# Fifth gate pair as split products inside attention, and the softmax maximum taken off in the exponential

## The chip, the cores and the metric

The kernel runs on one core of a Trainium2 chip. The metric is the device time of one execution in microseconds (us). The kernel before takes 1711.48 us, the median of three runs that lie between 1711.03 and 1711.93.

The engines are named as in the profile: PE is the matrix engine (PEld its weight loads, which overlap its products), DVE the vector engine, ACT the scalar engine, POOL the general one, SP the engine that only starts transfers. Each engine runs its own instructions in the order in which they are written, and waits at semaphores for the others.

## The reference

One decoder layer on 256 tokens of width 2048, all in fp32. What matters here is its first half:

```python
h = rms_norm(x, attn_norm_w)
q, k, v, z, gates = split(h @ w_in)              # gates: 2 x 2048 columns
# branch A: 16 query heads, 4 key heads, window 128, blocks of 128
scores = q @ k.T * 64**-0.5 - slope[head] * dist # -inf outside the window
m = max(max(scores, axis=-1), sink[head])
p = exp(scores - m)
attn = (p / (sum(p) + exp(sink[head] - m))) @ v
# branch B: RWKV-7 time mixing of z, gives y
merged = sigmoid(gates[0]) * (attn @ w_branch_a) + sigmoid(gates[1]) * (y @ w_branch_b)
x = x + merged @ w_out
x = x + moe(rms_norm(x))                         # 32 experts, two of them per token
out = rms_norm(x)
```

## The kernel before

**Stages.** The program goes once through these stages: x is transposed and normed to `hT`; the projections z, q, k, v, the small ones ("lora") and the first four of the eight gate pairs; attention, with the fifth gate pair laid between its steps; RWKV, once for each half of the heads, with gate pairs six to eight laid between its steps; the two branch products and `w_out`; routing; and the 32 experts, whose weights of 4 MB each stream in (three per expert).

**Gate pairs.** A gate pair is 512 of the 4096 gate columns for both blocks of 128 tokens (t = 0 and 1). It is a sum over 16 slices k of `hT`, so it has 32 products of 128x128 by 128x512. The weights arrive in chunks of eight slices in the slots of a ring. There are two ways to make such a product:

- Most projections run as split products: ACT copies a weight slice to fp32r (`hi`), DVE subtracts it from the slice (`lo`, written over the slice itself in the ring), and PE makes three fp32r products, hi with hi of h, hi with lo of h, lo with hi of h (`PRODUCTS`). Gate pairs six to eight are such; their slices are numbered y from 0, ACT's part is `f_hi` (L1566), DVE's `f_lo` (L1977), PE's `fill_mm` (L769). `hi` lies in eight buffers `f8`, which share their place with `hT`.
- The fifth gate pair is a plain fp32 product of `hT` and the slot, `gate_mm` (L747), with no work on ACT or DVE. The trace holds two PE records for each fp32 product.

Since `f8` lies over `hT`, `f_hi` waits until `gate_mm` has read `hT` for the last time (`chunk_used` at NF).

**Attention.** It has four units u, of eight heads and one block of 128 queries each. Units 0 and 1 see 128 keys, units 2 and 3 see 256. For each unit:

- PE `scores` (L786), into banks that unit u-2 has left
- DVE `shifted`: eight operations that add the slope (L1941), row maximum (L1944), maximum with the sink (L1945), sink minus maximum (L1946), scores minus maximum (L1947); it then signals `sm_done`
- ACT `exponentials`: one over all eight heads (L1532), one of 128x8 for the sinks
- DVE `normed`: sum, reciprocal, and one product over all heads (L1956 to L1959); it signals `pr_done`
- PE `turned` (transposes, L632), ACT `turned_out` (L1539), PE `values` (L808), ACT `values_out` (L1545)

PE's order was written by hand. DVE's is shifted 0, shifted 1, normed 0, shifted 2, normed 1, shifted 3, normed 2, normed 3, and then `f_lo` for y = 0 to 3. After the last `exponentials` ACT makes y = 0, then the two sigmoids of the fifth gate pair (`gate_out`, L1485, ahead of the first a table load, and behind each a store to DRAM), then `turned_out` of unit 2. The filling products of y = 0 reuse the banks of the fifth pair, so they wait for these sigmoids.

**Loads.** SP starts a load of the gate slices of pairs six to eight (L470, 1 MB each) when PE has read what lay in the slot.

Of the kernel before, what the change touches and what calls it, by code (L numbers as in the profile page):

```python
# [4 lines left out]
F32 = mybir.dt.float32  # L5
# [126 lines left out]
def hybrid_layer(nc, a, out):  # L132
    with ExitStack() as ctx:
# [25 lines left out]
        amax = sb("amax", [P, 8])  # L159
        aes2 = sb("aes", [P, 2, 8])  # L160
# [201 lines left out]
        F0 = UZ + UX  # L362
# [78 lines left out]
        def _(sp):  # L441
# [24 lines left out]
            for g in range(UF // 4):  # L466
                c = 2 * GD + 2 + g // 2
                s, o = slot_of(NG + c), 4 * (g % 2)
                sp.wait_ge(*((S("chunk_used"), NF - 1 + g // 2) if g < 4 else (S("w_used"), 4 + F0 + 4 * (g - 3))))
# [4 lines left out]
            for c in range(8):  # L474
                if c == 2:
                    sp.wait_ge(S("yc_done"), HALVES)
                sp.wait_ge(*((S("w_used"), 4 + F0 + UF - 8 + 8 * min(c, 1)) if c < 4 else (S("chunk_used"), NF + c - 3)))
# [12 lines left out]
            for c in range(8):  # L490
                sp.wait_ge(S("chunk_used"), NF + 5 + c if c < 2 else NF + 8 + c - 1)
# [3 lines left out]
                if 2 <= c < 6:  # L495
# [3 lines left out]
                    if c == 4:  # L499
                        sp.wait_ge(S("chunk_used"), NF + 8)  # L500
# [16 lines left out]
            for h in range(2):  # L517
                sp.wait_ge(S("chunk_used"), NF + 16 - 1 + h)
# [106 lines left out]
        def _(pe):  # L625
# [108 lines left out]
            gate_part = [0]  # L734

            def gate_mm(count):


                for m in range(gate_part[0], gate_part[0] + count):
                    k, t = divmod(m, TT)  # L740
                    n = NG + 2 * GD + k // 8
                    if k == 0:

                        pe.wait_ge(S("gate_out"), 2 * GD - 1 + t)
                    if t == 0 and k % 8 == 0:
                        full(n)
                    last = mm(ps[:, 6 + t, :], hT[:, k, 128 * t:128 * t + 128], slot(n)[:, k % 8, :],  # L747
                              start=k == 0, stop=k == KT - 1)
                    if t and k % 8 == 7:
                        last.then_inc(S("chunk_used"), 1)  # L750
                    elif k == KT - 1:
                        last.then_inc(S("gate_ps"), 1)
                gate_part[0] += count

            fill_part = [0]
# [60 lines left out]
            gate_mm(8)  # L816
            scores(2)
            gate_mm(1)
            turned(0)
            gate_mm(1)  # L820
            values(0)
            gate_mm(5)
            scores(3)
            gate_mm(1)
            turned(1)
            gate_mm(1)
            values(1)
            gate_mm(15)
# [249 lines left out]
            assert gate_part[0] == TT * KT and fill_part[0] == 2 * UF  # L1078
# [299 lines left out]
        def _(act):  # L1378
# [90 lines left out]

            gate_tile = [0]  # L1470
# [82 lines left out]
            turned_out(1)  # L1553
            values_out(1)
            exponentials(3)
            f_at = [0]

            def f_hi(upto):

# [886 lines left out]
```

## Time and profile before

| | us |
|---|---|
| median of 3 runs | 1711.48 |
| the profiled execution, its time | 1710.47 |
| its span in the trace | 1708.7 |
| busy in the span: PE / DVE / ACT | 1423.5 / 735.6 / 434.7 |

The span is the time between the first and last instruction of the trace; the execution's own time is 1.8 us more. All positions below are microseconds from the span's start. Attention runs from 329 to 384 us, RWKV from there to about 590, the experts from about 800 to the end. "Busy" of PE counts a product from its start to its modelled end, and products overlap, so the cost of one is read from the distance between starts: the length of a run of products over their number.

### The profile page before, as it was taken

What the parts mean: (1) busy time and instruction counts of PE and PEld (TensorE: products, weight loads), DVE (VectorE), ACT (ScalarE), POOL (GpSimd) and SP (SyncE); (2) the same over time, 40 slices, a digit from 0 to 9 for tenths busy, and PEclk for the clock granted to TensorE, in tenths of its full rate; (3) what the DMA queues carried; (4) which work ended last, traced back from release to release, by engine and by line L of the source; (5) the groups of instructions that cost most, each with busy time, mean ns of one, the idle gap of its engine ahead of it and who ended that gap; (6) DMA issues with size and microseconds to landing.
All of it is one profiled execution on the core that took longest, in us unless ns stands there. A gap on an engine that the chain in (4) does not pass through costs nothing.

```text
span 1708.7 us, 26529 instructions
## 1 busy us (share of the span) xinstructions
PE 1423.5 (83%) x11614; PEld 873.9 (51%) x11614; DVE 735.6 (43%) x1101; ACT 434.7 (25%) x601; POOL 49.3 (3%) x40
## 2 busy tenths in 40 slices
PE   7999999988899999999787686776776767767766
PEld 6888888757777788886232141232322322322322
DVE  6666554578476766553322232223231322322232
ACT  5444444345353434444100000000000000000002
POOL 3000000001103010000000000000000000000000
PEclk9999999999999999999888888888888888888888
DMA  9645456231231493858999999999999999999996
GB/s 349 222 175 185 150 205 225 75 111 52 65 94 43 176 340 123 335 208 350 423 433 432 429 433 433 432 432 431 432 432 432 433 431 430 433 433 431 432 427 291
DMA packets 80539, 529.31 MB, mean 310 GB/s; under 512 B 7840, under 2 KB 10154, under 8 KB 65866
## 3 DMA queue, kind: packets, MB, share of 16 engines
q1 hardware_dynamic: 75584, 514.50, 73.9%
q0 software_dynamic: 2224, 9.35, 1.5%
q10 hardware_dynamic: 2650, 4.26, 0.7%
q8 instruction: 66, 1.08, 0.3%
q14 instruction: 15, 0.12, 0.0%
HBM read 521.80 MB, written 6.29 MB: 309 GB/s over the span
## 4 chain that ended last, share of the span: by engine, by line
PE 51%; DMA 40%; DVE 5%; ACT 2%; issue 2%; DVEq 0%; SPq 0%; ACTq 0%
DMA ring<-in_expert_w_up 14%; DMA ring<-in_expert_w_gate 12%; PE ps L1084 10%; DMA ring<-in_expert_w_down 8%; PE ps L669 7%; PE ps L1193 7%; PE ps L730 5%; DMA arena<-in_expert_w_up 4%; PE ps L1329 3%; PE ps L670 3%; PE ps L769 3%; DMA arena<-in_expert_w_gate 2%; PE ps L747 1%; PE ps L632 1%; PE ps L1283 1%
## 5 line engine op out<-in xcount | busy, mean ns | idle before, releaser
L2291 DVE TENSOR_TENSOR arena<-arena,ps 128x512 f32<-128x512 f32 x248 | 154.0, 682 | 403.0 <-PE ps L1181 402.1
L1193 PE MATMUL ps<-ring,arena 128*32 128x512 f32 x1024 | 156.7, 763 | 93.1 <-DMA ring<-in_expert_w_gate 56.0
L1193 PE MATMUL ps<-arena 128*32 128x512 f32 x1018 | 149.0, 732 | 81.4 <-DMA arena<-in_expert_w_up 50.3
L669 PE MATMUL ps<-h_both,w_hi 128*128 128x512 f32 x544 | 194.6, 402 | 1.9 <-DVE w_lo L1857 1.9
L670 PE MATMUL ps<-h_both,w_lo 128*128 128x256 f32 x544 | 153.7, 283 | 0.0
L1193 PEld LDWEIGHTS ps<-ring,arena 128*32 128x32 f32 x1024 | 37.5, 134 | 207.5 <-issue 97.6
L1193 PEld LDWEIGHTS ps<-arena 128*32 128x32 f32 x1018 | 37.3, 130 | 181.5 <-issue 119.3
L669 PEld LDWEIGHTS ps<-h_both,w_hi 128*128 128x128 f32 x544 | 103.3, 190 | 28.3 <-DVE w_lo L1857 2.5
L1915 DVE TENSOR_TENSOR w_lo<-ring,w_hi 128x1024 fp32r<-128x1024 f32 (+1 forms) x62 | 74.4, 1199 | 82.7 <-ACT w_hi L1497 82.4
L1987 DVE TENSOR_TENSOR v_lo<-ring,v_hi 128x1024 fp32r<-128x1024 f32 x64 | 78.3, 1224 | 69.1 <-ACT v_hi L1527 68.7
L1716 ACT ACTIVATE arena<-ps 128x512 f32<-128x512 f32 x32 | 33.7, 1052 | 280.6 <-PE ps L1193 272.7
L670 PEld LDWEIGHTS ps<-h_both,w_lo 128*128 128x128 f32 x544 | 103.9, 191 | 0.0
L2335 DVE COPY arena<-ps 128x512 f32<-128x512 f32 x32 | 33.3, 1040 | 158.4 <-PE ps L1193 158.4
L1329 PE MATMUL ps<-arena 128*32 128x512 f32 x512 | 81.7, 796 | 22.4 <-DVE arena L2344 11.4
L1329 PE MATMUL ps<-ring,arena 128*32 128x512 f32 x512 | 79.9, 781 | 23.8 <-DMA ring<-in_expert_w_down 15.3
L1527 ACT ACTIVATE v_hi<-ring 128x1024 fp32r<-128x1024 f32 x64 | 67.8, 1063 | 98.5 <-PE ps L1084 98.5
L1497 ACT ACTIVATE w_hi<-ring 128x1024 fp32r<-128x1024 f32 (+1 forms) x62 | 64.2, 1040 | 81.4 <-PE ps L730 36.4
L1718 ACT ACTIVATE arena<-ps 128x256 f32<-128x256 f32 x32 | 12.3, 383 | 277.3 <-PE ps L632 277.3
L730 PE MATMUL ps<-w_hi,h_both 128*128 128x512 f32 x256 | 78.9, 389 | 0.0
L1283 PE MATMUL ps<-cst,arena 128*128 128x32 f32 x512 | 63.3, 277 | 16.3 <-ACT arena L1718 15.1
L1857 DVE TENSOR_TENSOR w_lo<-ring,w_hi 128x1024 fp32r<-128x1024 f32 x48 | 58.4, 1238 | 38.4 <-ACT w_hi L1443 37.8
L1181 PE MATMUL ps<-arena 32*128 32x512 f32 x512 | 73.8, 639 | 0.7 <-ACT arena L1725 0.7
(341 smaller groups left out, 2125.6 us busy)
## 6 DMA issues: line engine op xcount, KB each, us to landing
arena<-in_expert_w_gate SPq DMA_DIRECT2D x15, 4096.0 KB, 32.7
ring<-in_expert_w_gate SPq DMA_DIRECT2D x15, 4096.0 KB, 32.8
arena<-in_expert_w_up SPq DMA_DIRECT2D x15, 4096.0 KB, 32.3
arena<-in_expert_w_down SPq DMA_DIRECT2D x15, 4096.0 KB, 33.4
ring<-in_w_in SPq DMA_DIRECT2D x28, 2048.0 KB, 7.7
ring<-in_expert_w_up SPq DMA_DIRECT2D x14, 4096.0 KB, 33.4
ring<-in_expert_w_down SPq DMA_DIRECT2D x14, 4096.0 KB, 34.3
ring<-in_w_out SPq DMA_DIRECT2D x8, 2048.0 KB, 8.2
```

The source lines that it names most:

```text
L669: mm(out, hi[:, 128 * n:128 * n + 128], both(k), start=start and n == 0, stop=False)
L670: last = mm(out[:, 0:TOK], lo[:, 128 * n:128 * n + 128], hf(0, k), start=False, stop=stop and n == 7)
L730: last = mm(ps[:, GD_BANK[b] + t, :], hf(v, 2 * n + i, 128 * t, 128), (hi, lo)[w][:, 512 * i:512 * i + 512], start=n == 0 and i == 0 and p ...
L1084: last = mm(ps[:, bank + t, :], left[x][:, k, 128 * t:128 * t + 128], late_pieces(buf)[w][:, 512 * n:512 * n + 512], start=start and n == ...
L1181: last = mm(ps[:, banks[nb], :], CTB[32 * nb:32 * nb + 32, 128 * t:128 * t + 128], YS[32 * nb:32 * nb + 32, :], start=not onto, stop=stop, ...
L1193: last = mm(ps[32 * c:32 * c + 32, bank, :], XS[:, k, 32 * j:32 * j + 32], w[c], start=i == 0, stop=i == 3, tile_position=(0, 32 * c))
L1283: last = mm(ps[:, 3, 128 * m + 32 * k:128 * m + 32 * k + 32], (GC, UC)[m][:, 128 * k:128 * k + 128], C("fold"), start=True, stop=True)
L1329: last = mm(ps[32 * nb:32 * nb + 32, 2, :], HIDT[:, 32 * k:32 * k + 32], place(3 * j + 2)[:, 2048 * k + 512 * nb:2048 * k + 512 * nb + 512 ...
L1527: f(late_pieces(y % 3)[0], src, ACT.Copy).then_inc(S("v_hi"), 1)
L1915: v.tensor_tensor(lo, src, hi.bitcast(F32), ALU.subtract).then_inc(S("w_lo"), 1)
L1987: v.tensor_tensor(lo, v_piece(y)[1], hi.bitcast(F32), ALU.subtract).then_inc(S("v_lo"), 1)
L2291: last = v.tensor_tensor(xs, xs, ps[:, banks[nb], :], ALU.add)
```

## The change

The fifth gate pair becomes a split product like the later three. Its slices are numbered y = -16 to -1, `gate_mm` is gone, and `fill_mm` stands wherever it stood, with the same counts. `hT` is now dead from the start of attention on, so `hi` of the new slices can be made there early. The first eight (y = -16 to -9) are made by ACT and DVE behind the last projection slices, ahead of attention's first softmax. The other eight stand between the steps of the softmax, and y = 0, which follows them, has moved ahead of `normed` of unit 3 on DVE. A buffer of `f8` is free again when PE has used the slice that is eight back.

In `shifted`, the subtraction over all scores (L1947) goes. In its place the negated maximum of each head is written as a 128x8 tile `nmax`, and ACT makes one exponential per head with that column as bias, so eight instructions where one was.

The waits of SP and ACT that counted `chunk_used` of the fifth pair now count `w_used`, at the same products of PE.

```diff
@@ -359,7 +360,9 @@
         NO = NM + 8
         NE = NO + 8
         UF = (8 - GD - 1) * KT
-        F0 = UZ + UX
+        UY = KT
+        F0 = UZ + UX + UY
+        ND = NG + 2 * GD
         UPG = 3 * GE
         EW = 2 * SLOT
 
@@ -466,7 +469,7 @@
             for g in range(UF // 4):
                 c = 2 * GD + 2 + g // 2
                 s, o = slot_of(NG + c), 4 * (g % 2)
-                sp.wait_ge(*((S("chunk_used"), NF - 1 + g // 2) if g < 4 else (S("w_used"), 4 + F0 + 4 * (g - 3))))
+                sp.wait_ge(S("w_used"), 4 + F0 + (8 * (g // 2 - 1) if g < 4 else 4 * (g - 3)))
                 sp.dma_start(ring[:, s, 512 * o:512 * o + 2048].rearrange("p (k n) -> p k n", k=4),
                              cols(GA0 + 512 * (c // 2), c % 2, 512)[:, o:o + 4, :]).then_inc(f_sem(g), 16)
             wa = a["w_branch_a"][0].rearrange("(k p) n -> p k n", p=P)
...
@@ -813,19 +795,19 @@
             pe.wait_ge(S("gate_out"), 4)
             scores(0)
             scores(1)
-            gate_mm(8)
+            fill_mm(8)
             scores(2)
-            gate_mm(1)
+            fill_mm(1)
             turned(0)
-            gate_mm(1)
+            fill_mm(1)
             values(0)
-            gate_mm(5)
+            fill_mm(5)
             scores(3)
-            gate_mm(1)
+            fill_mm(1)
             turned(1)
-            gate_mm(1)
+            fill_mm(1)
             values(1)
-            gate_mm(15)
+            fill_mm(15)
             turned(2)
             fill_mm(FILL_A)
             values(2)
...
@@ -1467,6 +1449,22 @@
                 act.wait_ge(S("zs_done"), 5 + 24 + t + 1)
                 f(lz[0:m, t, :], zs[0:m, t, :], ACT.Copy, scale=omm[0:m, t:t + 1]).then_inc(S("za_done"), 1)
 
+            f_at = [-UY]
+
+            def f_hi(upto):
+
+
+                for y in range(f_at[0], max(upto, f_at[0])):
+                    if y < 0 and y % 8 == 0:
+                        n = NF + y // 8
+                        act.wait_ge(S(f"slot_full{n % RING}"), 16 * (n // RING + 1))
+                    elif y >= 0 and y % 4 == 0:
+                        act.wait_ge(f_sem(y // 4), f_landed(y // 4))
+                    if y >= 8 - UY:
+                        act.wait_ge(S("w_used"), 4 + F0 + y - 7)
+                    f(f_pieces(y)[0], f_src(y), ACT.Copy).then_inc(S("w_hi"), 1)
+                f_at[0] = max(upto, f_at[0])
+
             gate_tile = [0]
 
             def gate_out():
@@ -1477,8 +1475,7 @@
                 if b < GD:
                     act.wait_ge(S("w_used"), 4 + UZ + UQ + UL + 8 * b + 8)
                 else:
-                    act.wait_ge(*((S("gate_ps"), b + 1 - GD) if t == 0 else (S("chunk_used"), NF) if b == GD else
-                                  (S("w_used"), 4 + F0 + KT * (b - GD))))
+                    act.wait_ge(*((S("gate_ps"), b + 1 - GD) if t == 0 else (S("w_used"), 4 + F0 + KT * (b - GD))))
                 if q >= 2:
 
                     act.wait_ge(S(f"gate_stored{t}"), 16 * b)
@@ -1511,6 +1508,8 @@
                         act.wait_ge(S("z_done"), 4 + 27)
                     gate_out()
                     gate_out()
+                if x == UX:
+                    f_hi(8 - UY)
             act.wait_ge(S("z_done"), 4 + 27)
             f(lz[0:64, 0, :], lz[0:64, 0, :], ACT.Tanh).then_inc(S("lora_done"), 1)
             f(lz[:, 1, :], lz[:, 1, :], ACT.Sigmoid).then_inc(S("lora_done"), 1)
@@ -1529,7 +1528,9 @@
             def exponentials(u):
 
                 act.wait_ge(S("sm_done"), u + 1)
-                f(probs_of(u), probs_of(u), ACT.Exp).then_inc(S("ex_done"), 1)
+                for h in range(8):
+                    last = f(probs_of(u)[:, h, :], probs_of(u)[:, h, :], ACT.Exp, bias=nmax2[:, u % 2, h:h + 1])
+                last.then_inc(S("ex_done"), 1)
                 f(aes2[:, u % 2, :], aes2[:, u % 2, :], ACT.Exp).then_inc(S("ex_done"), 1)
 
             def turned_out(u):
@@ -1547,26 +1548,15 @@
 
             exponentials(0)
             exponentials(1)
+            f_hi(-4)
             turned_out(0)
             values_out(0)
+            f_hi(-1)
             exponentials(2)
             turned_out(1)
             values_out(1)
+            f_hi(0)
             exponentials(3)
-            f_at = [0]
-
-            def f_hi(upto):
-
-
-                for y in range(f_at[0], max(upto, f_at[0])):
-                    if y % 4 == 0:
-                        act.wait_ge(f_sem(y // 4), f_landed(y // 4))
-                    if y >= 8:
-                        act.wait_ge(S("w_used"), 4 + F0 + y - 7)
-                    f(f_pieces(y)[0], f_src(y), ACT.Copy).then_inc(S("w_hi"), 1)
-                f_at[0] = max(upto, f_at[0])
-
-            act.wait_ge(S("chunk_used"), NF)
             f_hi(1)
             gate_out()
             gate_out()
@@ -1929,6 +1919,20 @@
 
             dve.wait_ge(S("const_in"), 16)
             dve.wait_ge(S("small_in"), 16 * 9)
+
+            f_at = [-UY]
+
+            def f_lo(upto):
+
+
+                for y in range(f_at[0], max(upto, f_at[0])):
+                    hi, lo = f_pieces(y)
+                    dve.wait_ge(S("w_hi"), F0 + y + 1)
+                    v.tensor_tensor(lo, f_src(y), hi.bitcast(F32), ALU.subtract).then_inc(S("w_lo"), 1)
+                f_at[0] = max(upto, f_at[0])
+
+            f_lo(8 - UY)
+
             def shifted(u):
 
                 n, hg = divmod(u, 2)
@@ -1944,7 +1948,7 @@
                 step(v.tensor_reduce(amax[:, :], probs, AX.X, ALU.max))
                 step(v.tensor_tensor(amax[:, :], amax[:, :], sink[:, 8 * hg:8 * hg + 8], ALU.max))
                 step(v.tensor_tensor(aes, sink[:, 8 * hg:8 * hg + 8], amax[:, :], ALU.subtract))
-                v.tensor_tensor(probs, probs, rep(amax[:, :], w), ALU.subtract).then_inc(S("sm_done"), 1)
+                v.tensor_scalar(nmax2[:, u % 2, :], amax[:, :], -1.0, None, ALU.mult).then_inc(S("sm_done"), 1)
 
             def normed(u):
 
@@ -1963,20 +1967,12 @@
             normed(0)
             shifted(2)
             normed(1)
+            f_lo(-1)
             shifted(3)
+            f_lo(0)
             normed(2)
+            f_lo(1)
             normed(3)
-            f_at = [0]
-
-            def f_lo(upto):
-
-
-                for y in range(f_at[0], max(upto, f_at[0])):
-                    hi, lo = f_pieces(y)
-                    dve.wait_ge(S("w_hi"), F0 + y + 1)
-                    v.tensor_tensor(lo, f_src(y), hi.bitcast(F32), ALU.subtract).then_inc(S("w_lo"), 1)
-                f_at[0] = max(upto, f_at[0])
-
             f_lo(4)
             dve.wait_ge(S("pv_ps"), 4)
 
```

PE, attention, from the scores of units 0 and 1 (L786) to `values` of unit 0 (L808; L632 is `turned`). Before:

```order
L786 MATMUL ps<-arena 128x128 x16
L747 MATMUL ps<-ring,arena 128x512 x8
L786 MATMUL ps<-arena 128x256 x8
L747 MATMUL ps<-ring,arena 128x512
L632 MATMUL ps<-cst,arena 128x128 x8
L747 MATMUL ps<-ring,arena 128x512
L808 MATMUL ps<-arena 64x128 x8
L747 MATMUL ps<-ring,arena 128x512 x5
```

Now, from `scores` of unit 2 on (L768 is `scores`, L751 the filling products, L635 `turned`, L790 `values`):

```order
L768 MATMUL ps<-arena 128x256 x8
L751 MATMUL ps<-f_hi,h_both 128x512 x2
L751 MATMUL ps<-ring_lo,h_both 128x512
L635 MATMUL ps<-cst,arena 128x128 x8
L751 MATMUL ps<-f_hi,h_both 128x512 x2
L751 MATMUL ps<-ring_lo,h_both 128x512
L790 MATMUL ps<-arena 64x128 x8
L751 MATMUL ps<-f_hi,h_both 128x512 x2
L751 MATMUL ps<-ring_lo,h_both 128x512
```

The places are the same; one fp32 product, two records in the trace, has become three fp32r products.

ACT, same stretch, from the exponentials of unit 0 (L1532, L1533) over `turned_out` and `values_out` (L1539, L1545) to those of unit 2. Before:

```order
L1532 ACTIVATE arena<-arena 128x1024
L1533 ACTIVATE aes<-aes 128x8
L1532 ACTIVATE arena<-arena 128x1024
L1533 ACTIVATE aes<-aes 128x8
L1539 ACTIVATE arena<-ps 128x1024
L1545 ACTIVATE arena<-ps 128x4x128
L1532 ACTIVATE ring<-ring 128x2048
L1533 ACTIVATE aes<-aes 128x8
```

Now (L1465 is `f_hi`, L1532 and L1534 the exponentials, L1540 and L1546 `turned_out` and `values_out`):

```order
L1532 ACTIVATE arena<-arena,nmax 128x128 x8
L1534 ACTIVATE aes<-aes 128x8
L1532 ACTIVATE arena<-arena,nmax 128x128 x8
L1534 ACTIVATE aes<-aes 128x8
L1465 ACTIVATE f_hi<-ring 128x512 x4
L1540 ACTIVATE arena<-ps 128x1024
L1546 ACTIVATE arena<-ps 128x4x128
L1465 ACTIVATE f_hi<-ring 128x512 x3
L1532 ACTIVATE ring<-ring,nmax 128x256 x8
L1534 ACTIVATE aes<-aes 128x8
L1540 ACTIVATE arena<-ps 128x1024
```

Each exponential of unit u has become eight, and seven slices of `hi` stand ahead of `turned_out` of unit 0 and ahead of the exponentials of unit 2. The first eight stand further up, ahead of the last two sigmoids of the projection stage:

```order
L1494 ACTIVATE w_hi<-ring 128x1024 x5
L1465 ACTIVATE f_hi<-ring 128x512 x8
L1482 ACTIVATE rs<-ps,rstd 128x512
L1485 DMA gate_spill<-rs 128x512
L1482 ACTIVATE rs<-ps,rstd 128x512
L1485 DMA gate_spill<-rs 128x512
```

DVE, from `shifted` of unit 3 (its first operation L1941, its subtraction L1947) to `f_lo` (L1977). Before:

```order
L1941 SCALAR_TENSOR_TENSOR ring<-cst,ps 128x256 x8
L1944 TENSOR_REDUCE amax<-ring 128x8
L1945 TENSOR_TENSOR amax<-amax,sink 128x8
L1946 TENSOR_TENSOR aes<-sink,amax 128x8
L1947 TENSOR_TENSOR ring<-ring,amax 128x2048
L1956 TENSOR_REDUCE asum<-ring 128x8
L1957 TENSOR_TENSOR asum<-asum,aes 128x8
L1958 RECIPROCAL asum<-asum 128x8
L1959 TENSOR_TENSOR ring<-ring,asum 128x2048
```

Now (L1931 is `f_lo`, L1945 and L1951 begin and end `shifted`):

```order
L1931 TENSOR_TENSOR ring_lo<-ring,f_hi 128x512 x7
L1945 SCALAR_TENSOR_TENSOR ring<-cst,ps 128x256 x8
L1948 TENSOR_REDUCE amax<-ring 128x8
L1949 TENSOR_TENSOR amax<-amax,sink 128x8
L1950 TENSOR_TENSOR aes<-sink,amax 128x8
L1951 TENSOR_SCALAR nmax<-amax 128x8
L1931 TENSOR_TENSOR ring_lo<-ring,f_hi 128x512
L1960 TENSOR_REDUCE asum<-ring 128x8
L1961 TENSOR_TENSOR asum<-asum,aes 128x8
L1962 RECIPROCAL asum<-asum 128x8
L1963 TENSOR_TENSOR ring<-ring,asum 128x2048
L1931 TENSOR_TENSOR ring_lo<-ring,f_hi 128x512
```

The subtraction over 2048 columns has become an operation on 8, and slices of `lo` stand ahead of, within and behind: seven, one and one.

## Rows read from the trace of the kernel before

**Rows 1.** Windows view: us, busy (x) of PE, PEld, DVE, ACT, POOL; PEclk, DMA share, GB/s.

```profile
329.00:372.00 43.00, 40.26 (x193) 21.58 (x192) 39.79 (x65) 15.83 (x21) 0.00 (x0) 1.00 0.21 69
800.00:1708.00 908.00, 658.96 (x4572) 251.03 (x4564) 250.94 (x465) 79.91 (x138) 0.57 (x1) 0.86 0.99 424
```

**Rows 2.** Chain that ended last, 300 to 480 us: start, us, what.

```profile
299.98 29.24 PE ps L730 x129
...
338.32 1.24 DVE arena L1947
...
343.56 1.03 ACT arena L1539
...
354.12 1.03 ACT arena L1539
...
356.29 13.09 PE ps L747 x30
...
370.05 1.28 ACT L1485
...
373.58 1.95 ACT ring L1539 x2
375.57 2.03 PE ps L808 x32
```

**Rows 3.** Timeline of PE: start, us, group, [idle before <-releaser].

```profile
331.13 7.13 PE L747 MATMUL ps<-ring,arena 128*128 128x512 f32 x16
339.60 2.00 PE L786 MATMUL ps<-arena 64*128 64x256 f32 x16 [1.34 <-DVE arena L1947]
...
369.20 1.91 PE L632 MATMUL ps<-cst,ring 128*128 128x128 f32 x16
```

**Rows 4.** Timeline of DVE in the attention stage, same columns.

```profile
330.46 1.67 DVE L1941 SCALAR_TENSOR_TENSOR arena<-cst,ps 128x128 f32<-128x128 f32 x8 [7.05 <-PE ps L786]
...
333.62 0.17 DVE L1946 TENSOR_TENSOR aes<-sink,amax 128x8 f32<-128x8 f32 x1
333.82 1.23 DVE L1947 TENSOR_TENSOR arena<-arena,amax 128x1024 f32<-128x1024 f32 x1
334.97 1.67 DVE L1941 SCALAR_TENSOR_TENSOR arena<-cst,ps 128x128 f32<-128x128 f32 x8
...
339.46 1.21 DVE L1956 TENSOR_REDUCE asum<-arena 128x8 f32<-128x1024 f32 x1
...
342.29 2.73 DVE L1941 SCALAR_TENSOR_TENSOR ring<-cst,ps 128x256 f32<-128x256 f32 x8
...
347.78 2.29 DVE L1947 TENSOR_TENSOR ring<-ring,amax 128x2048 f32<-128x2048 f32 x1
...
360.51 2.28 DVE L1956 TENSOR_REDUCE asum<-ring 128x8 f32<-128x2048 f32 x1
...
365.66 2.29 DVE L1956 TENSOR_REDUCE asum<-ring 128x8 f32<-128x2048 f32 x1
...
384.86 3.70 DVE L1977 TENSOR_TENSOR ring_lo<-ring,f_hi 128x512 fp32r<-128x512 f32 x6
```

**Rows 5.** Timeline of ACT, same columns.

```profile
329.25 0.69 ACT L1485 ACTIVATE rs<-ps,rstd 128x512 f32<-128x512 f32 x1 [7.10 <-PE ps L730]
...
335.08 1.06 ACT L1532 ACTIVATE arena<-arena 128x1024 f32<-128x1024 f32 x1 [1.27 <-DVE arena L1947]
...
350.11 1.91 ACT L1532 ACTIVATE ring<-ring 128x2048 f32<-128x2048 f32 x1 [3.73 <-DVE ring L1947]
...
384.20 3.22 ACT L1566 ACTIVATE f_hi<-ring 128x512 fp32r<-128x512 f32 x6
...
389.87 1.57 ACT L1586 ACTIVATE arena<-ps,vecT 128x256 f32<-128x256 f32 x4 [1.53 <-PE ps L873]
```

**Rows 6.** Source view of L470 on SP's queue, 340 to 400 us.

```profile
DMA to landing us min/median/max: 4.9/5.1/8.8
```

**Rows 7.** Timeline of SP's queue.

```profile
353.24 43.26 SPq L470 DMA_DIRECT2D ring<-in_w_in  x5
```

More of the change, by code:

```diff
@@ L159, in hybrid_layer @@
         amax = sb("amax", [P, 8])
+        nmax2 = sb("nmax", [P, 2, 8])
         aes2 = sb("aes", [P, 2, 8])
@@ L476, in _ @@
                     sp.wait_ge(S("yc_done"), HALVES)
-                sp.wait_ge(*((S("w_used"), 4 + F0 + UF - 8 + 8 * min(c, 1)) if c < 4 else (S("chunk_used"), NF + c - 3)))
+                sp.wait_ge(*((S("w_used"), 4 + F0 + UF - 8 + 8 * min(c, 1)) if c < 4 else (S("chunk_used"), ND + c - 3)))
                 sp.dma_start(ring[:, c % RING, :].rearrange("p (k n) -> p k n", k=8),
@@ L490, in _ @@
             for c in range(8):
-                sp.wait_ge(S("chunk_used"), NF + 5 + c if c < 2 else NF + 8 + c - 1)
+                sp.wait_ge(S("chunk_used"), ND + 5 + c if c < 2 else ND + 8 + c - 1)
                 sp.dma_start(ring[:, c % 2, :].rearrange("p (k n) -> p k n", k=8),
@@ L499, in _ @@
                     if c == 4:
-                        sp.wait_ge(S("chunk_used"), NF + 8)
+                        sp.wait_ge(S("chunk_used"), ND + 8)
                     w = eg if c < 4 else eu
@@ L517, in _ @@
             for h in range(2):
-                sp.wait_ge(S("chunk_used"), NF + 16 - 1 + h)
+                sp.wait_ge(S("chunk_used"), ND + 16 - 1 + h)
                 sp.dma_start(place(2)[:, SLOT * h:SLOT * h + SLOT], ed[:, 0, SLOT * h:SLOT * h + SLOT]).then_inc(S("place2"), 16)
@@ L732, in _ @@
                 last.then_inc(S("w_used"), 1)
[L734 to L755, printed above, removed]
+            fill_part = [-TT * UY]
             def fill_mm(count):
@@ L1076, in _ @@
                 mm(ps[:, 3, 0:256], C("ident"), cst[:, 0:256], start=True, stop=True)
-            assert gate_part[0] == TT * KT and fill_part[0] == 2 * UF
+            assert fill_part[0] == 2 * UF
             def late_unit(left, buf, bank, ks, start, stop):
```

## The prediction, made before the change was timed

> **What bounds the kernel now.** First I read the two windows [rows 1]. In the expert stage the DMA share is 0.99: it ends when the last of a fixed number of bytes has come, so it ends earlier only if it starts earlier. In attention nothing streams (share 0.21), PE is busy 40.3 of 43 us and DVE 39.8, ACT only 15.8. So two engines are nearly full at once, and relieving one alone would give little. PE's clock is granted in full there (1.00, the level of 2.4 GHz).
>
> Then the chain of waits says who is last where [rows 2]. At the start DVE is: `scores` of unit 2 (339.60) waits for the subtraction of unit 1, which starts at 338.32 [rows 2, 3]. From there to 369.38 PE is, the last 13.09 us of it as one run of `gate_mm`. Then ACT is: a table load at 370.05, two sigmoids, and only at 373.58 `turned_out` of unit 2, so that `values` of unit 2 starts at 375.57. What follows (`values`, `turned_out`, RWKV) goes from engine to engine in an order that the change leaves alone, and so should move as a block with that 375.57. That start is the number to forecast.
>
> **The cost of each part.** One pair (slice, token block):
>
> - Before: 13.09 us for 30 records is 0.436 each, and two records make a product: 0.873 us [rows 2].
> - Now: the split products of the projection run at 29.24/129 = 0.227 us each, three are 0.68 [rows 2]. Each pair gives back 0.19 us, all 32 give 6.2 us of PE.
> - Each slice costs ACT 3.22/6 = 0.54 us for hi [rows 5] and DVE 3.70/6 = 0.62 for lo [rows 4]. Of the 16 slices eight are hidden: ACT is idle for 7.10 us before 329.25, so from 322.15, and 8 x 0.54 = 4.3; DVE is idle for 7.05 before 330.46, so from 323.41, and 8 x 0.62 = 5.0 ends at 328.4 [rows 4, 5]. Without that cover they would cost up to 5 us, in the open on DVE. The other eight add 5.0 us to DVE in attention.
> - The four subtractions go: 1.23 twice and 2.29 twice, 7.0 us; four of 128x8 take their place, which I price as L1946, 0.17 each [rows 4]. DVE's balance is -7.0 + 0.7 + 5.0 = -1.3 us, small beside PE's.
> - The exponentials. The trace has no 128-column one with a bias. Its nearest row is L1586, four of 256 columns with a bias column, 0.39 us each; a column costs (1.91 - 1.06)/1024 = 0.83 ns, so 128 columns cost 0.39 - 0.11 = 0.285 [rows 5]. Eight are 2.3 us for units 0 and 1 (was 1.06) and 3.1 for units 2 and 3 (was 1.91). The bounds are taken up below.
>
> The Trainium skill (ScalarE: Activation LUTs, section What ACT_TABLE_LOAD costs) has for an ACTIVATE with a pointer bias about 280 ns plus 0.833 ns a column, of which 93 ns overlap when they come back to back. By that, 0.29 and 0.40 us, eight would be 2.4 and 3.2 us, and the sum would be the same within 0.2 us. It speaks against the change so far as it makes the fixed part be paid eight times; the row L1586 bears the overlapped figure out.
>
> **The walk.** Now the three queues, each step after what it waits for. DVE first, with its own rows as lengths [rows 4], `shifted` 0 ready at 333.82 + 0.17 = 334.0:
>
> - `shifted` 1: 338.32 - 334.97 = 3.35, + 0.17: 337.5 (was 339.55)
> - `normed` 0: 342.29 - 339.46 = 2.83: 340.35. Its exponentials ran 334.0 to 336.5.
> - `shifted` 2: 347.78 - 342.29 = 5.49, + 0.17: 346.0
> - `normed` 1, 2.83: 348.85; seven slices of lo, 4.3: 353.15; `shifted` 3, 5.66: 358.8; one slice: 359.4
> - `normed` 2: 365.66 - 360.51 = 5.15: 364.6 (was 365.66)
> - one slice, `normed` 3: 370.35 (was 370.8)
>
> PE: the eight pairs behind 331.13 end at 336.6, so `scores` of unit 2 waits for DVE until 337.5, 2.1 us earlier than before. From there to `turned_out` of unit 0 it was 343.56 - 339.60 = 3.96 us [rows 2, 3], now 0.2 less, 341.3. But ACT has the exponentials of unit 1 (to 340.0) and four slices of hi (to 342.1) ahead of it: 0.8 us late. From `scores` 2 to `turned_out` of unit 1 it was 354.12 - 339.60 = 14.5 us [rows 2, 3] with eight pairs; now 14.5 - 1.55 + 0.8: 351.3. On ACT the exponentials of unit 2 stand behind the hi of y = -2, whose buffer comes free with the fourth of five pairs, 347.2; they end near 351.2, just in time. From `turned_out` 1 to the end of the pairs it was 369.38 - 354.12 = 15.26 us with 15 pairs [rows 2], now 12.4: PE is done at 363.7. Short runs between other work cost some 0.1 us more each, so I take 363.9, 5.5 us earlier.
>
> `turned` of unit 2 then waits for `normed` 2 at 364.6: PE's gain is cut by DVE from 5.5 to 4.7 us. It takes 1.9 us [rows 3] and ends at 366.6.
>
> ACT: before, hi of y = 0 stood between the gate and the table load. Now ACT has done the exponentials of unit 3 at 362.1 and that slice at 362.7. Its load is issued with the 16th pair, about 350.5 (was 353.24), and lands 4.9 to 8.8 us later [rows 6, 7], in time. The first block's sum is ready one pair before 363.9, at 363.2. From table load to `turned_out` 2 it was 373.58 - 370.05 = 3.53 [rows 2]: 366.75, as the transposes end. So this part goes under the transposes, worth another 2 us. `turned_out` 2 starts at 366.8 instead of 373.58 and `values` 2 at 368.8 instead of 375.57, 6.8 us earlier; `turned` 3 follows at 370.8, behind `normed` 3 (370.35).
>
> Semaphore latencies between three engines this close to each other will eat some: I take **6.5 us**. The profiled time of 1710.47 would become 1704.0. Against the median, which is 1.0 us above that execution, it is 1711.48 - 6.5 = **1705.0 us**.
>
> **Bounds.** Exponentials: below, as a copy without bias (0.54 at 512 columns gives 0.22 and 0.32), PE is earlier, but DVE holds `turned` 2: at most 0.3 us more gain. Above, the lone 512-column sigmoid, 0.69 us each [rows 5]: worked out with the rivals. lo on DVE: half of a subtraction of 1024 columns, 1.23 us, is 0.61 too [rows 4], so I leave 0.1 a slice open: `normed` 2 later by 0.8 us. The operation of 128x8 cannot cost less than nothing: 0.7 us more gain at most. PE's short runs: 0.2 more each over five runs is 1.0, of which 0.7 is slack behind DVE.
>
> **The rivals.**
>
> *Exponentials do not overlap.* If each paid 0.1 us more (0.385 and 0.49), `turned_out` 0 would be 0.8 us later and the exponentials of unit 2 another 0.8: PE's pairs end at 365.5, the sigmoids follow at 368.3, the gain is 5.2 us: 1706.3. At 0.2 us more it is about 3.6: 1707.9. For it speaks that none with a bias of this width is in the trace; against it that L1586 overlaps.
>
> *DVE alone decides.* If the first eight slices of lo or the y = -8 to -1 find hi late (ACT waits there for buffers), DVE has holes. Two us of holes ahead of `normed` 2 give 4.8 us: 1706.7.
>
> *Given back.* If something after 375 keeps its old time (a load in RWKV, the first expert weights), the gain shrinks to nothing: 1711.5. SP's loads are issued by PE's progress [rows 6, 7], which speaks against it.
>
> *Slower.* ACT becomes the bound of attention. At 0.69 us each, exponentials of unit 0 end at 339.7, of unit 1 at 345.4, four hi at 347.5, so `turned_out` 0 is 6.2 us late, those of unit 2 end at 357.8, and PE's pairs at 370.4; with ACT's sigmoids behind it `turned_out` 2 is at 373.2, 0.4 us before the old one. So the point where it turns is 0.7 us for each of the 32; at 0.9 us, 16 more steps of 0.2 on the path (units 1 and 2) make it 3 us slower: 1714.3. Nothing in the trace is that slow at 256 columns.
>
> **How the numbers follow.** Chances: the forecast 0.72 (gain 5.8 to 7.5), more than that 0.05 (to 8.5), exponentials or DVE dearer 0.14 (gain 3.5 to 5.8, and a little below), given back 0.05, slower 0.04. Less than 0.2%, 3.4 us, can't be told from no change. So faster 0.89, same 0.07, slower 0.04. The range of 1703.3 to 1707.9 takes in the forecast and the dearer exponentials, and leaves out some 2 in 10.
>
> **What would show it.** In the new profile: split products at 0.68 us a pair in attention; eight exponentials in 2.3 and 3.1 us; eight hi and lo finished before 329; `scores` of unit 2 at 337.5; `turned` of unit 2 at 364.7 released by DVE, not by PE's own queue; no gap between it and the filling products for the sigmoids; `values` of unit 2 at 368.8; and every later stage earlier by as much. It is wrong if ACT releases PE more than once before 364, if the exponentials take over 3 us for 128 columns, or if the expert stage starts at its old time.

## The result, and the profile after

The changed kernel takes 1702.11 us (median of 5 runs, 1698.25 to 1703.30), the kernel before 1711.48 (median of 5, 1708.75 to 1712.13): ratio 0.9943, 95% interval 0.9929 to 0.9956, so 9.4 us faster, where 6.5 was forecast. It lies 1.2 us below the lower end of the range, 1703.3. With the later runs of the same pair the spread is wider: 17 runs of the change have a mean of 1701.6 (1697.4 to 1705.0), 65 of the kernel before 1710.9 (1705.1 to 1717.3). The difference of these means is 9.3 us, 1.1 either way (95%, from the spread of the single runs). One run of an experiment below (split products alone) took 2230.24 us at a mean granted clock of 0.638, where the others of that kernel had 0.912 to 0.917; it is left out of all means.

The trace's span is 1700.3 us (1708.7 before), the execution's own time 1702.1. First the chain that ended last (start, us, what), to be read beside [rows 2]:

```profile
299.88 24.71 PE ps L733 x109
324.59 1.12 PE ps L768 x16
...
333.05 2.14 ACT arena L1532 x7
335.28 2.08 ACT f_hi L1465 x4
337.37 0.91 ACT arena L1540
338.32 1.09 PE ps L790 x16
...
346.84 1.03 ACT arena L1540
...
349.01 10.65 PE ps L751 x45
359.67 1.76 PE ps L635 x16
361.45 1.95 ACT ring L1540 x2
363.44 2.03 PE ps L790 x32
```

PE's timeline at the first `scores` (start, us, group), here and before:

```profile
324.52 2.06 PE L768 MATMUL ps<-arena 64*128 64x128 f32 x32
```

```profile
329.14 2.06 PE L786 MATMUL ps<-arena 64*128 64x128 f32 x32
```

So 4.6 us are gained before the first changed instruction is on the path. That is no part of the forecast, and has experiments of its own below. Positions inside attention are therefore best counted from the first `scores`. `values` of unit 2 starts 363.44 - 324.52 = 38.92 us after them; before it was 375.57 - 329.14 = 46.43 [rows 2]. Attention gave 7.5 us.

To set the walk beside the trace, add 4.62 to each position. The pairs end at 359.67, which is 364.3 (forecast 363.9), `turned_out` of unit 2 starts at 361.45, which is 366.1 (366.8), `values` of unit 2 at 363.44, which is 368.1 (368.8). The table load and the sigmoids are gone from the chain. The wait of `turned_out` of unit 0 for ACT is there: exponentials of unit 1, four slices of hi, then `turned_out` at 337.37. By 4.62 more that is 342.0, where the walk had 342.1. `values` of unit 0 had to wait 0.96 us for it, `values` of unit 1 0.41 us for the next one (0.25 us each before).

DVE's queue, its timeline (start, us, group, idle before), beside [rows 4]:

```profile
319.11 4.91 DVE L1931 TENSOR_TENSOR ring_lo<-ring,f_hi 128x512 fp32r<-128x512 f32 x8 [0.32 <-ACT f_hi L1465]
325.73 1.67 DVE L1945 SCALAR_TENSOR_TENSOR arena<-cst,ps 128x128 f32<-128x128 f32 x8 [1.72 <-PE ps L768]
...
329.09 0.17 DVE L1951 TENSOR_SCALAR nmax<-amax 128x8 f32<-128x8 f32 x1
329.17 1.67 DVE L1945 SCALAR_TENSOR_TENSOR arena<-cst,ps 128x128 f32<-128x128 f32 x8
...
332.53 0.17 DVE L1951 TENSOR_SCALAR nmax<-amax 128x8 f32<-128x8 f32 x1
...
343.84 4.29 DVE L1931 TENSOR_TENSOR ring_lo<-ring,f_hi 128x512 fp32r<-128x512 f32 x7
...
356.98 2.29 DVE L1963 TENSOR_TENSOR ring<-ring,asum 128x2048 f32<-128x2048 f32 x1
359.19 0.68 DVE L1931 TENSOR_TENSOR ring_lo<-ring,f_hi 128x512 fp32r<-128x512 f32 x1
```

The first eight slices of lo are done at 324.0, before `scores` start. nmax of unit 1 (332.53) lets `scores` of unit 2 start at 332.76, 8.24 us after the first ones; it was 10.46. `normed` of unit 2 ends at 359.27.

ACT's, beside [rows 5]:

```profile
317.43 4.26 ACT L1465 ACTIVATE f_hi<-ring 128x512 fp32r<-128x512 f32 x8
...
329.30 2.46 ACT L1532 ACTIVATE arena<-arena,nmax 128x128 f32<-128x128 f32 x8
...
342.98 3.29 ACT L1532 ACTIVATE ring<-ring,nmax 128x256 f32<-128x256 f32 x8
...
357.69 1.28 ACT L1482 ACT_TABLE_LOAD   x1
...
361.45 1.94 ACT L1540 ACTIVATE ring<-ps 128x1024 f32<-128x1024 f32 x2 [0.56 <-PE ps L635]
```

Eight exponentials of 128 columns take 2.46 us and eight of 256 take 3.29; forecast were 2.3 and 3.1. One by itself lasts 0.39 and 0.50 us, so eight end to end would be 3.1 and 4.0: they overlap by some 0.09 us each. The table load starts at 357.69, while PE still has pairs to do, and `turned_out` of unit 2 waits 0.56 us for the transposes, no longer for ACT's own sigmoids. PE at that place:

```profile
359.27 0.40 PE L751 MATMUL ps<-ring_lo,h_both 128*128 128x512 f32 x1
359.50 1.91 PE L635 MATMUL ps<-cst,ring 128*128 128x128 f32 x16
361.17 0.71 PE L751 MATMUL ps<-f_hi,h_both 128*128 128x512 f32 x2
```

The last product starts 0.23 us ahead of the transposes, one product's length, so PE did not wait for DVE; and the filling products follow the transposes at once.

### The profile page after: what moved, and what is told of

The parts are those of the page before. It is cut to its first block, busy times and chain, and to the rows that moved or that the text cites. A ratio compares the mean times of both kernels' runs of the same rounds, so it can differ in the third digit from the quotient of the medians.

```text
span 1700.3 us, 26655 instructions
## 1 busy us (share of the span) xinstructions
PE 1419.5 (83%) x11646; PEld 880.2 (52%) x11646; DVE 737.7 (43%) x1117; ACT 447.7 (26%) x645; POOL 48.8 (3%) x40
## 4 chain that ended last, share of the span: by engine, by line
PE 50%; DMA 41%; DVE 5%; ACT 2%; issue 2%; DVEq 0%; SPq 0%; ACTq 0%
DMA ring<-in_expert_w_up 15%; DMA ring<-in_expert_w_gate 15%; PE ps L1066 10%; DMA ring<-in_expert_w_down 8%; PE ps L672 7%; PE ps L1175 6%; PE ps L733 5%; PE ps L751 4%; PE ps L673 4%; PE ps L1311 3%; DMA arena<-in_expert_w_up 2%; PE ps L635 1%; PE ps L1155 1%; PE ps L966 1%; PE ps L1265 1%
## 5 line engine op out<-in xcount | busy, mean ns | idle before, releaser
L1175 PE MATMUL ps<-ring,arena 128*32 128x512 f32 x1024 | 158.1, 769 | 90.7 <-DMA ring<-in_expert_w_gate 54.2
L672 PE MATMUL ps<-h_both,w_hi 128*128 128x512 f32 x544 | 191.1, 395 | 0.9 <-DVE w_lo L1847 0.8
L673 PE MATMUL ps<-h_both,w_lo 128*128 128x256 f32 x544 | 153.0, 281 | 0.0
L672 PEld LDWEIGHTS ps<-h_both,w_hi 128*128 128x128 f32 x544 | 102.9, 189 | 24.4 <-DVE w_lo L1847 1.5
L1311 PE MATMUL ps<-ring,arena 128*32 128x512 f32 x512 | 84.1, 816 | 23.5 <-DMA ring<-in_expert_w_down 15.0
L673 PEld LDWEIGHTS ps<-h_both,w_lo 128*128 128x128 f32 x544 | 103.7, 191 | 0.0
L751 PE MATMUL ps<-f_hi,h_both 128*128 128x512 f32 x256 | 84.3, 410 | 0.2 <-ACT rs L1482 0.2
```

Of the source, the lines that this page charges most:

```text
L672: mm(out, hi[:, 128 * n:128 * n + 128], both(k), start=start and n == 0, stop=False)
L673: last = mm(out[:, 0:TOK], lo[:, 128 * n:128 * n + 128], hf(0, k), start=False, stop=stop and n == 7)
L751: last = mm(ps[:, 6 + t, :], hf(v, k, 128 * t, 128), f_pieces(y)[w], start=k == 0 and p == 0, stop=k == KT - 1 and p == 2)
L1175: last = mm(ps[32 * c:32 * c + 32, bank, :], XS[:, k, 32 * j:32 * j + 32], w[c], start=i == 0, stop=i == 3, tile_position=(0, 32 * c))
L1311: last = mm(ps[32 * nb:32 * nb + 32, 2, :], HIDT[:, 32 * k:32 * k + 32], place(3 * j + 2)[:, 2048 * k + 512 * nb:2048 * k + 512 * nb + 512 ...
```

## The experiments

"Attention" is the distance from the first `scores` to `values` of unit 2 in the trace: 46.43 us before, 38.92 in the change. It repeats within 0.02 us in every trace of the same kernel. The last column compares means of the runs made on the same occasion (for the change, of all its runs); what stands in brackets is the 95% interval to either side. The run of the kernel before that belongs to the two single runs, of e9 and e11, took 1713.13 us.

| | attention, us | pair in projection loop, us | mean time against before, us |
|---|---|---|---|
| before, three traces | 46.42 to 46.43 | 0.353, 0.353, 0.353 | |
| change, three traces | 38.91 to 38.92 | 0.347, 0.347, 0.347 | -9.3 (1.1) |
| split products alone (e5) | 48.03 | 0.347 | +0.7 (2.5) |
| softmax alone (e6) | 45.02 | 0.347 | -1.8 (1.8) |
| e9, no cover | 48.23 | 0.353 | one run, 1713.87 |
| e11, sigmoids behind | 41.17 | 0.347 | one run, 1705.30 |
| two hi earlier (e10, e14) | 38.79 | 0.353, 0.347 | -9.3 (2.9), e14 |

### Each half alone (e5, e6)

Split products with the old softmax: in the changed kernel

```diff
-                for h in range(8): last = f(...[:, h, :], ACT.Exp, bias=nmax2[:, u % 2, h:h + 1])
+                f(probs_of(u), probs_of(u), ACT.Exp).then_inc(S("ex_done"), 1)
-                v.tensor_scalar(nmax2[:, u % 2, :], amax[:, :], -1.0, None, ALU.mult)
+                v.tensor_tensor(probs, probs, rep(amax[:, :], w), ALU.subtract)
```

> The changed kernel with the old softmax (subtraction over all scores on DVE, one exponential), so only the split products of the fifth gate pair are new. By the walk of the prediction DVE now has 5 us more and nothing less: normed of unit 2 is ready near 370.6 against 365.66 (in the positions of the kernel before), PE waits for it, the hidden sigmoids give back 2 us, and values of unit 2 starts about 45.4 us after the first scores (46.4 before, 38.9 in the change): attention gains 1 us. Rival, PE alone counts: 5 to 6 us gained, 41 us. Ahead of attention: if the pace of the projection (0.353 or 0.347 us a pair) goes with PE's program, this has 0.347 and L733's stretch starts near 238; time 1706. If it goes with ACT's and DVE's program, 0.353 and 1709.

The new softmax with the fifth pair in fp32: the same lines the other way round in the kernel before.

> The kernel before with the new softmax alone (maximum as bias of one exponential per head), the fifth gate pair in plain fp32. By the walk the wait of scores of unit 2 for DVE goes (2.1 us), PE's pairs are then last everywhere, and the eight exponentials lie beside them: values of unit 2 starts 44.3 us after the first scores (46.4 before), attention gains 2 us. Rival, exponentials too slow: no gain or a loss, 46 to 49. Ahead of attention: if the pace of the projection goes with PE's program, 0.353 and L730's stretch near 242, time 1708; if with ACT's, 0.347, near 238, time 1704.

Attention lost 1.6 us with the first and won 1.4 with the second; together they win 7.5. Of the split products alone, PE's timeline (start, us, group, idle before), then DVE's where it waits for the slow `scores`, and windows of 4 us (us; busy of PE, PEld, DVE, ACT, POOL; granted clock of PE; DMA share; GB/s):

```profile
336.46 3.57 PE L768 MATMUL ps<-arena 64*128 64x256 f32 x16 [2.54 <-DVE arena L1949]
...
368.22 3.68 PE L635 MATMUL ps<-cst,ring 128*128 128x128 f32 x16 [3.30 <-DVE ring L1961]
```

```profile
340.08 2.73 DVE L1943 SCALAR_TENSOR_TENSOR ring<-cst,ps 128x256 f32<-128x256 f32 x8 [0.85 <-PE ps L768]
```

```profile
336.00:340.00 4.00, 3.54 (x17) 2.56 (x17) 3.13 (x5) 3.23 (x6) 0.00 (x0) 0.57 0.00 0
368.00:372.00 4.00, 3.78 (x17) 3.78 (x18) 3.90 (x6) 0.38 (x2) 0.00 (x0) 0.50 1.02 354
```

DVE's queue is 5 us longer and releases PE twice, after 2.54 and 3.30 us of waiting. In both places PE's granted clock falls to the lower of its two levels, 1.2 GHz: 0.57 and 0.50 in these windows, against 1.00 in the window of attention of before, where PE's one long wait was 1.34 us [rows 1, 3]. So `scores` of unit 2 take 3.57 us instead of 2.00, and the transposes of unit 2 take 3.68 instead of 1.91 [rows 3]. These are 1.57 and 1.77 us more. Of the first only the 0.85 us count for which DVE then waited, as DVE is last from there to the transposes. Without 0.85 and 1.77 attention would be 48.03 - 2.62 = 45.4 us by this estimate, which is what was expected from the walk, and the walk had no clock in it. PE's 6.2 us came to nothing as DVE had more to do, and what the sigmoids gave back went to the clock.

The chain that ended last with the new softmax alone (start, us, what):

```profile
328.30 7.06 PE ps L748 x16
335.36 1.93 PE ps L787 x16
...
351.98 13.09 PE ps L748 x30
...
369.27 1.95 ACT ring L1542 x2
...
371.26 2.03 PE ps L809 x32
```

Here PE's fp32 pairs (L748) are last from the first `scores` on: `scores` of unit 2 starts when the eight pairs are over, 9.05 us after the first, so only 1.4 of the 2.1 us are won, and the run of 13.09 us stands as before. Both halves together win more than their sum: each engine's relief is worth something only with the other's.

### Taking the cover away (e9)

```diff
-                if x == UX: f_hi(8 - UY)
+            f_hi(8 - UY)
             exponentials(0)
```

> The changed kernel with the first eight slices of hi made by ACT behind the sigmoids and the three small activations, not ahead of them; DVE's eight lo stay ahead of the first softmax and wait for them. It takes the cover away. Theory of the prediction (the eight are hidden by idle time, DVE is nearly last in attention): the first operation of shifted comes 7.3 us later and all of DVE's queue with it, values of unit 2 starts 46 us after the first scores instead of 38.9, time 1709. Rival (slack in attention takes it up): 39 to 42 us.

Its chain that ended last (start, us, what):

```profile
331.62 4.91 DVE ring_lo L1930 x8
336.53 1.59 DVE arena L1944 x8
...
343.45 3.79 PE ps L768 x16
...
372.05 1.76 PE ps L635 x16
...
375.83 2.03 PE ps L790 x32
```

DVE's eight slices of lo (L1930) are now in the chain, and `shifted` of unit 0 starts at 336.53, 8.9 us after the first `scores` (327.60) instead of 1.2. PE waits twice. First for lo, and here its clock stays up (1.00 from 332 to 338 us):

```profile
332.37 0.73 PE L751 MATMUL ps<-f_hi,h_both 128*128 128x512 f32 x2 [2.71 <-DVE ring_lo L1930]
```

Then for 5.24 us ahead of `scores` of unit 2, and now it is down (0.50 from 343 to 347 us): they take 3.79 us, where the chain of e6 above has 1.93. `values` of unit 2 comes 9.3 us later than in the change, where 7 were expected and the prediction had put the cover at up to 5. `scores` of unit 2 is 7.6 us later: 4.9 for lo, and the rest because ACT's hi now stands behind its sigmoids and small activations, which the prediction's 5 us did not hold. The clock adds 1.8.

### Sigmoids behind the transposes (e11)

```diff
+            act.wait_ge(S("pt_ps"), 3)
             gate_out()
             gate_out()
```

> The changed kernel with the two sigmoids of the fifth gate pair made to wait until the transposes of unit 2 are done, so that they can't go under them. Theory of the prediction (the sigmoids' 3.5 us from table load to turned_out went under PE's pairs and transposes): turned_out of unit 2 comes 3.4 us later, values of unit 2 starts 42.3 us after the first scores instead of 38.9. Rival (they never were on the path): 38.9 to 40.

ACT's timeline at the place (start, us, group, idle before):

```profile
358.94 1.28 ACT L1482 ACT_TABLE_LOAD   x1 [1.36 <-issue]
361.36 0.69 ACT L1482 ACTIVATE rs<-ps,rstd 128x512 f32<-128x512 f32 x1 [1.14 <-PE ps L635]
...
362.50 0.69 ACT L1482 ACTIVATE rs<-ps,rstd 128x512 f32<-128x512 f32 x1 [0.46 <-ACT rs L1482]
...
363.60 1.94 ACT L1540 ACTIVATE ring<-ps 128x1024 f32<-128x1024 f32 x2 [0.40 <-ACT rs L1482]
```

The table load starts ahead of the added wait (358.94), so it stays hidden; the two sigmoids alone come into the open, and `turned_out` at 363.60 is 2.2 us later than in the change. Attention is 2.25 us longer, not the 3.4 expected with the load. So the sigmoids under the transposes are worth 2.2 us, as the prediction had it (2), and the load lies beside work anyway.

### What is last now (e10)

```diff
             exponentials(0)
+            f_hi(-6)
             exponentials(1)
```

> The changed kernel with two of the four slices of hi moved from behind the exponentials of unit 1 to ahead of them, where ACT is idle for 0.89 us. Theory: turned_out of unit 0 comes 1.0 us earlier, PE's wait of 0.96 us ahead of values of unit 0 goes, PE's pairs end 1 us earlier, but DVE's normed of unit 2 (ready 0.3 us before PE needs it) then holds turned: 0.3 us gained, values of unit 2 starts 38.6 us after the first scores. Rival (PE alone is last): 1 us gained, 37.9.

The chain that ended last in e10:

```profile
357.13 2.21 DVE asum L1961
...
359.80 2.30 DVE ring L1964
...
362.15 1.98 PE ps L635 x16
...
366.14 2.03 PE ps L790 x32
```

PE's wait went, but DVE's `normed` of unit 2 (L1961 to L1964) released the transposes at 362.15, and `values` of unit 2 came 0.13 us earlier than in the change. PE and DVE are now last within 0.2 us of each other. Its time cannot be told from that of the change.

### The microseconds ahead of attention

The projection loop is the same in all programs, and its pairs of products (L669 and L670, L672 and L673 in the change) came every 0.353 us before and every 0.347 us in the change. First, the tile nmax moves all tiles behind it by 64 bytes. It was added unused to the kernel before (e2), and taken out of the change (e3), beside repeats of both (e1, e4):

```diff
         amax = sb("amax", [P, 8])
+        pad = sb("pad", [P, 16])
```

```diff
-        nmax2 = sb("nmax", [P, 2, 8])
+        nmax2 = rs[:, 1200:1216].rearrange("p (a n) -> p a n", a=2)
```

> The kernel before, unchanged, looked at once more. In its first trace the pairs of products L669/L670 of the projection came every 0.353 us, in that of the change every 0.348 us, with the same instructions, and 4.6 us were gained ahead of attention. If that pace belongs to the run (theory: chance), this trace may show either pace. If it belongs to the program (theory: place in SBUF), it shows 0.353 again, L730's stretch starts near 242 us, and the span is within 2 us of 1708.7.

> The kernel before with one unused tile of 64 bytes per partition (128x16) where the change puts its tile nmax, so that all tiles behind it, the arena with h_both and w_hi too, lie 64 bytes further on, as in the change. Theory place in SBUF: the pairs of the projection come every 0.348 us instead of 0.353, L730's stretch starts near 237.5, and the time is 3 to 5 us below before (1707). Rival, chance: no difference that repeats, 1711.5. Rival, program size or instruction fetch: no difference either, as the instructions are the same.

> The changed kernel with nmax laid into free columns of the tile rs, so that no tile moves against the kernel before. Theory place in SBUF: the projection has the old pace of 0.353 us, attention keeps its gain (values of unit 2 starts 38.9 us after the first scores, 46.4 before), and the time is 1711.5 - 7 = 1704.5, or 1704 to 1706. Rival, chance: as the change, 1702.

> The changed kernel once more, on the same chip as the others. Theory place in SBUF: 1702 and the pace of 0.348 us again, 2 to 5 us below the version without the moved tiles. Rival, chance: the same time as that version within 1.5 us.

The padded kernel had 0.353 and was 1.0 us (1.6 to either side) slower than before; the change without the moved tile had 0.347 and was 9.4 us (2.1) faster. So the place in SBUF makes no difference that these runs show. Next, the length of the programs, by empty instructions in a branch that is never entered, on PE (e7) and on ACT (e8):

```diff
+                for _ in range(64): pe.nop()
```

```diff
+                for _ in range(32): act.nop()
```

> The kernel before with 64 empty PE instructions in the branch for full experts, which these inputs never enter; nothing that runs is changed. PE's program is then as much longer as in the change. Theory, length of PE's program sets the pace of the projection loop: 0.347 us a pair, L730's stretch starts near 238, time 1707. Rival, it is the code that runs or chance: 0.353, 242, time 1710.5.

> The kernel before with 32 empty ACT instructions in the branch for full experts, never entered; nothing that runs is changed. So far four programs with the kernel before's attention on ACT had 0.353 us a pair in the projection loop, and five with a changed one 0.347. Theory, length of ACT's program (or where it lies) sets that pace: 0.347 here, L730's stretch starts near 238.5. Rival, chance or something else: 0.353 and 242 (chance: either).

PE's gave 0.353 (0.3 us slower than before, 1.3 to either side), ACT's 0.347 (single runs of 1709.53 and, in e15, 1707.84), which looked like an answer; but e9 and e10 changed ACT's program again and had 0.353. So four kernels were repeated:

> The kernel before for the third time. Both traces so far have 0.353 us a pair in the projection loop. Theory, the pace is fixed for a program (whatever fixes it): 0.353 again, L730's stretch near 242 us. Rival, it falls by chance at each execution: either pace, and over these four repeats about half differ from what the same kernel showed before.

> The changed kernel for the third time, timed again. Both traces so far have 0.347 us a pair. Fixed for a program: 0.347 again and a time 9 to 10 us below before (7.5 in attention, 2 to 3 ahead of it). Chance: either pace, and over many runs the time is 7.5 us below before. Attention itself: values of unit 2 starts 38.9 us after the first scores either way.

> The version with two slices of hi ahead of the exponentials of unit 1, for the second time, now timed. Its trace had 0.353 us a pair, the change has 0.347. Fixed for a program: 0.353 again, and a time 2 us above the change's. Chance: either pace, and the change's time less 0.1 us.

> The kernel before with 32 empty ACT instructions in a branch never entered, for the second time. Its trace had 0.347 us a pair. Fixed for a program: 0.347 again, L730's stretch near 239. Chance: either.

Three repeated themselves (0.353, 0.347, 0.347), and e14 did not. One program, timelines of PE, fifteen pairs apart: e10 early in its loop, e10 later, and e14 later.

```profile
30.21 0.39 PE L672 MATMUL ps<-h_both,w_hi 128*128 128x512 f32 x1
...
35.41 0.39 PE L672 MATMUL ps<-h_both,w_hi 128*128 128x512 f32 x1
```

```profile
110.18 0.40 PE L672 MATMUL ps<-h_both,w_hi 128*128 128x512 f32 x1
...
115.48 0.40 PE L672 MATMUL ps<-h_both,w_hi 128*128 128x512 f32 x1
```

```profile
110.32 0.39 PE L672 MATMUL ps<-h_both,w_hi 128*128 128x512 f32 x1
...
115.52 0.39 PE L672 MATMUL ps<-h_both,w_hi 128*128 128x512 f32 x1
```

These are 5.20, 5.30 and 5.20 us for 15 pairs. So the same program can have either pace, and so can one execution: in nine of the 17 traces the pace changes, four times to the slower and five times to the faster one, eight times between 46 and 54 us, where PE mostly has a short wait for DVE, and once near 29. From 60 to 200 us it never changes, and the paces named here are those. Of the 17 traces, 7 had the slower and 10 the faster. Whether a program leans to one of them stays open: the kernel before showed the slower three times in three, the change the faster three times in three; by even chance such a split comes once in 32.

The pace is not all that moves ahead of attention. The third trace of before (e12) has the slower pace too, but its first `scores` start at 326.98, 2.2 us ahead of the first trace's: PE's first pairs, at the lower clock and mostly 0.64 us each, are fewer (5 for 8), and the wait of 0.81 us at 52.51 is missing.

What may come from here can be read from all traces together. With the code of before ahead of attention (before, e1, e2, e7, e8, e12, e15) the first `scores` start at 324.55 to 329.14, mean 327.6; with that of the change (the change, e3, e4, e9, e10, e11, e14, e13) at 324.42 to 327.60, mean 325.5. That is 2.2 us earlier, 1.8 either way. The timed runs don't settle it: e2 and e7 (slower pace) lie within 1 us of before, and so does e5 (faster pace), whose attention is 1.6 us longer; and the pace is known only of the one run with a trace.

## Why the prediction was wrong

- *PE's pairs*: forecast were 0.68 us a pair and 0.1 more for short runs; the chain has 10.65 for 15, 0.71 each. The pairs end 0.4 us behind the forecast. Right, but priced a little too low.
- *The cover of the first eight*: right that they are hidden, hi at 321.7, lo at 324.0. Its price without cover was named too low (5, measured 9.3 in e9): the clock (1.8) and the place of hi behind ACT's other work were left out.
- *Exponentials*: right, 2.46 and 3.29 for 2.3 and 3.1. The fixed part does overlap. The estimate that the prediction worked out from the Trainium skill (ScalarE: Activation LUTs, What ACT_TABLE_LOAD costs), 2.4 and 3.2 us, lies nearer to these than the one from my row.
- *DVE*: the mechanism is right, the sum mis-sized. nmax was priced at 0.17 us at the end of `shifted`, but the next instruction starts 0.08 us behind its start (329.09, 329.17). `normed` of unit 2 ends 34.75 us after the first `scores` instead of the forecast 35.5. Four times 0.09 us at nmax are some 0.4 of these 0.7; the rest is a tenth each at the start of `shifted`, in the seven slices of lo and in `normed` itself. So PE did not wait ahead of the transposes of unit 2, where 0.7 was expected, and they were not released by DVE, as the prediction had it. In e10, where DVE is last, its `normed` of unit 2 ends at the same 34.75.
- *Sigmoids under the transposes*: right, 2.2 us (e11) for 2.
- *"I take 6.5 us"*: here a step failed. The walk gave 6.8, and 0.3 was taken off for latencies that its own rows already held; the trace has 7.5, by the 0.7 of DVE. That is still inside the range: 1711.48 - 7.5 is 1704.0.
- *"What follows ... should move as a block", and nothing else counts*: this is the step that put the time outside the range. The forecast summed attention alone, put everything outside it at nothing, without a reason for what lies ahead of it, and took the bounds of the range from costs of attention alone. Of the measured 9.3 us (1.1 either way) 7.5 are shown to be attention's, and 1.8 lie outside it. Behind attention the block did move: from `values` of unit 2 to the end it takes 1335.3 us on the mean of the seven traces of before's code and 1335.3 on that of the eight of the change's. Ahead of attention those of the change are 2.2 us earlier (1.8 either way), which is the size of the 1.8. Why, stays open: no changed instruction is on the path there, and whether it is chance or goes with the program is not settled. The range also had no room for how runs scatter: the 17 runs of the change lie up to 7.5 us apart and the 65 of before 12.2, where the three runs I had lay within 0.9.
- *The signs of being wrong*: one of them came, "if ACT releases PE more than once before 364". ACT released it twice (`values` of units 0 and 1, after 0.96 and 0.41 us). It did so before the change too (0.25 each), and the walk held the first one, so this was a badly chosen sign and not a failure of the sum.
- The rivals (exponentials that don't overlap, holes on DVE, given back, slower) did not come. "Given back" is out: the trace is 12.1 us ahead at `values` of unit 2 and 11.3 when the first expert's down weights are asked for (757.37 before, 746.06 now). From there to the end it took 951.3 us in the first trace of before and 953.8 in each of the two others, in the three of the change 954.2, 954.2 and 952.4; it was the first trace of before that was quick there.

## What to carry to other kernels

Where two engines are both over nine tenths busy, don't drop a relief that gives little alone: here one lost 1.6 us, the other won 1.4, and both together won 7.5. A wait that a change adds on PE can cost its length and then half of PE's clock for the next steps, and on the path this counts only as far as the next engine has to wait for it. Work that fills an engine's idle time just ahead of a tight stage can be worth more than its own length when it is lost, as its predecessors come into the open with it. And before giving a range, look how far runs of one kernel lie apart over many executions, not over three, and how far the stages that the change leaves alone do.

## What the runs showed of the hardware

PE's pair of an fp32r product of 512 columns and one of 256, with their weight loads and at a granted clock of 1.00, has two steady paces, 0.353 and 0.347 us, kept from 60 to 200 us; one program showed both, and nine executions changed from one to the other before 54 us. After waits of 2.54, 3.30 and 5.24 us in attention the granted clock fell to its lower level, and the next sixteen products or transposes took 1.8 to 1.9 times as long; after one of 1.34 it did not, and after one of 2.71 (e9) it did not either. So the length of the wait alone does not decide it. That this clock has two levels, 1.2 and 2.4 GHz, is what the Trainium skill says (TensorE: Matmul & The Clock Gate, Part 1), and the rows agree: a stretch that is all at one level shows 0.50 or 1.00. A 128x8 operation on DVE lasts 0.17 us, but the next one that does not depend on it starts 0.08 us after its start (329.09, 329.17). An exponential of 128 columns lasts 0.39 us and eight in a row 2.46.
